# The two output tiles of a weight chunk: tile by tile, or in turn at every matmul

## The reference

```
proj = xn @ w_in                                  # 2048 x 4096, and w_o 2048 x 2048
h = gelu(conv(xn @ w_g)) * (xn @ w_u)             # 2048 x 6144 each, in both layers
f = h @ w_d                                       # 6144 x 2048, in both layers
```

## Time and profile before

| what | value |
|---|---|
| three runs | 2781.56, 2787.35, 2787.73 us (median 2787.35) |
| the profiled execution, first to last instruction | 2787.2 us |
| PE busy | 2630.7 us, 94%, 20425 matmuls |
| PEld busy | 2488.0 us, 89%, 20425 loads |
| DVE busy | 1648.2 us, 59% |
| ACT busy | 1121.7 us, 40% |
| chain that ended last | PE 85%, of it L1513, L1514 and L1515 24% each |

### The profile page before, as it was taken

How to read it: one execution, slowest core, us unless ns; L and a number is a source line. 1 busy time by engine, 2 the same in 40 slices (tenths; PEclk the granted TensorE clock), 3 DMA queues, 4 the chain that set the end, 5 groups by cost and what they waited for, 6 DMA issues and landing times.

```text
span 2787.2 us, 54670 instructions
## 1 busy us (share of the span) xinstructions
PE 2630.7 (94%) x20425; PEld 2488.0 (89%) x20425; DVE 1648.2 (59%) x2583; ACT 1121.7 (40%) x1531; POOL 252.7 (9%) x337
## 2 busy tenths in 40 slices
PE   5988979999999999997889999996999999999998
PEld 5988979999999999997886556896999999999997
DVE  5889567654666466648642214448665566556655
ACT  4366344443443344435423222334443344334433
POOL 1043130000000000022300000022000000000012
PEclk9999989999999999998989999998999999999999
DMA  6534535555555555553413330152555555555552
GB/s 202 182 126 147 187 121 159 181 183 180 180 180 182 180 177 180 181 168 108 120 55 110 94 106 17 64 179 96 185 180 180 179 179 180 183 176 179 180 185 75
DMA packets 435802, 425.46 MB, mean 153 GB/s; under 512 B 37308, under 2 KB 424468, under 8 KB 435432
## 3 DMA queue, kind: packets, MB, share of 16 engines
q1 hardware_dynamic: 432088, 415.63, 47.8%
q0 software_dynamic: 3200, 6.06, 0.7%
q10 hardware_dynamic: 432, 2.66, 0.3%
HBM read 420.86 MB, written 3.95 MB: 152 GB/s over the span
## 4 chain that ended last, share of the span: by engine, by line
PE 85%; DVE 8%; issue 3%; POOL 2%; ACT 1%; SPq 0%; DMA 0%; DVEq 0%; POOLq 0%; ACTq 0%
PE acc L1513 24%; PE acc L1514 24%; PE acc L1515 24%; PE mis L1750 2%; PE mis L1772 2%; DVE lo L1002 2%; DVE f L1224 2%; DVE ssum L1014 1%; PE acc L1740 1%; PE mis L1751 1%; ACT hi L693 1%; PE mis L1821 1%; DVE xnl L1031 1%; PE mis L1820 1%; POOL aa L614 0%
## 5 line engine op out<-in xcount | busy, mean ns | idle before, releaser
L1002 DVE TENSOR_TENSOR lo<-raw,hi 128x1024 fp32r<-128x1024 f32 x752 | 908.4, 1224 | 830.0 <-ACT hi L693 829.1
L693 ACT ACTIVATE hi<-raw 128x1024 fp32r<-128x1024 f32 x752 | 786.2, 1055 | 930.8 <-PE acc L1515 928.7
L1513 PE MATMUL acc<-xnh,hi 128*128 128x264 f32 x3664 | 1057.3, 289 | 65.7 <-issue 29.8
L1515 PE MATMUL acc<-xnh,lo 128*128 128x264 f32 x3664 | 1053.3, 287 | 0.0
L1514 PE MATMUL acc<-xnl,hi 128*128 128x264 f32 x3664 | 1051.7, 287 | 0.0
L1513 PEld LDWEIGHTS acc<-xnh,hi 128*128 128x128 f32 x3664 | 703.9, 192 | 71.6 <-issue 47.0
L1514 PEld LDWEIGHTS acc<-xnl,hi 128*128 128x128 f32 x3664 | 703.8, 192 | 0.4
L1515 PEld LDWEIGHTS acc<-xnh,lo 128*128 128x128 f32 x3664 | 699.3, 191 | 0.0
L1513 PE MATMUL acc<-hh,hi 128*128 128x264 f32 x2112 | 602.3, 285 | 0.0
L1515 PE MATMUL acc<-hh,lo 128*128 128x264 f32 x2112 | 602.2, 285 | 0.0
L1514 PE MATMUL acc<-hl,hi 128*128 128x264 f32 x2112 | 601.1, 285 | 0.0
(11 more groups left out here) (292 smaller groups left out, 2242.6 us busy)
## 6 DMA issues: line engine op xcount, KB each, us to landing
raw<-in_w_ffn_g SPq DMA_DIRECT2D x192, 512.0 KB, 4.5
raw<-in_w_ffn_u SPq DMA_DIRECT2D x192, 512.0 KB, 4.3
raw<-in_w_ffn_d SPq DMA_DIRECT2D x192, 512.0 KB, 3.7
raw<-in_w_rg_in SPq DMA_DIRECT2D x64, 512.0 KB, 5.1
raw<-in_w_rg_o SPq DMA_DIRECT2D x32, 512.0 KB, 4.6
cpage<-in_cache_kv_latent SPq DMA_DIRECT2D x64, 256.0 KB, 2.5
raw<-in_w_mla_o SPq DMA_DIRECT2D x32, 512.0 KB, 3.4
raw<-in_w_dkv SPq DMA_DIRECT2D x8, 512.0 KB, 4.6
```

Of the source, the lines that this page charges most:

```text
L693: act.activation(hi[:, c % SPLIT, :, 0:n], raw[:, c % RAW, :, 0:n], ACT.Copy).then_inc(s.hi_ready, 1)
L1002: dve.tensor_tensor(lo[:, c % SPLIT, :, 0:n], raw[:, c % RAW, :, 0:n], hi[:, c % SPLIT, :, 0:n].bitcast(F32), ALU.subtract).then_inc(s.lo_ ...
L1513: pe.matmul(out, wh, xh, start=start, stop=False)
L1515: return pe.matmul(out, wl, xh, start=False, stop=stop)
```

## The change

The three passes are written out in `group`, and the loop over the two output tiles becomes the innermost. The same 24 matmuls are issued for a chunk, with the same weights, activations and banks, and for each bank in the same order; only how the two tiles' matmuls are interleaved differs. The calls of `mm3` outside `group` stay as they are.

```
-                    for m in range(tiles):
-                        for k in range(4):
-                            kk = 4 * q + k
-                            w = (slice(None), slot, k, slice(m * P, m * P + P))
-                            last = mm3(acc[2 * (g % 2) + m][:, 0:T], hi[w], lo[w], xh[:, kk, :], xl[:, kk, :],
-                                       start=kk == 0, stop=kk == 4 * n - 1)
+                    for k in range(4):
+                        kk = 4 * q + k
+                        for n_pass, (half, moving) in enumerate(((hi, xh), (hi, xl), (lo, xh))):
+                            for m in range(tiles):
+                                w = (slice(None), slot, k, slice(m * P, m * P + P))
+                                last = pe.matmul(acc[2 * (g % 2) + m][:, 0:T], half[w], moving[:, kk, :],
+                                                 start=kk == 0 and n_pass == 0,
+                                                 stop=kk == 4 * n - 1 and n_pass == 2)
                     last.then_inc(s.chunk_used, 1)
```

## The result

| | median us | lowest to highest | runs |
|---|---|---|---|
| before | 2787.35 | 2781.56 to 2787.73 | 3 |
| changed | 2801.33 | 2799.72 to 2801.99 | 3 |

The changed kernel is slower by about 0.5%: ratio 1.0054, 95% interval 1.004 to 1.0068. That is 14.0 us more. I had forecast no change (2787 us) with 0.62, and slower with 0.17; the time lies inside the range that I gave (2770 to 2808).

The account below looks back on a forecast made before the run. TensorE's own matmul rate, 121.6 ns each, was taken to bound the kernel; 2787.2 us span + 0 + 0 + 0 gave 2787 us. Likeliest case 2779 to 2796, 8 in 10 range 2770 to 2808.

Parts of the forecast that it names:

- no change: Whole kernel: a time within 0.3% (8.4 us) of before, predicted as 2787 us; chance 0.62.
- slower: Whole kernel: more than 0.3% slower, by a worse pairing (0.15) or a falling clock (0.02); chance together 0.17.
- What bounds the kernel: Feed-forward stretches: only TensorE's rate counts, 121.6 ns per matmul, without gaps or waits, at clock 1.00.
- Instructions and waits at 0: Chunks in `group`: 17,568 matmuls and as many weight loads stay, no wait moves; cost 0.
- Bank switches at 0: Within chunks: 16,104 further bank switches cost 0, with -18 and +3 us kept as bounds.
- The three places: Bank evidence: a chunk's two existing switches, the float32 gate matmuls, and `value_pair`, which never switches; none showed a bank effect.
- Repeated weights at 0: L1513 to L1514: loading the same weights again saves nothing, so losing the repetition costs 0; at most 4 us gain.
- Which load lies beside which stream, at 0: Within chunks: new pairing of weight loads with streams taken as 0, bounded by -13 to +21 us.
- the two alternating patterns: Distances between matmul starts repeat every second chunk; both patterns sum to 2916 or 2917 ns, read as a stable mean.
- The worse pairing: Tile 1's weight load beside tile 0's stream makes each matmul 122.7 ns: +21 us, 2808 us; chance 0.15.
- The sum: Whole kernel: span 2787.2 us plus three zeros gives 2787 us, the span being 0.15 us from the median.
- The read ports: TensorE: by the skill's two independent read ports, loading weights takes no read bandwidth, so pairing would do nothing; 0.

Follow-up runs that it names:

- e1_bank: Kernel before, its order of weights and activations kept, but the bank alternates at each matmul; 2788.19 us, ratio 1.0003.
- e2_order: Changed kernel's order of weights and activations, but a chunk's first twelve matmuls write bank 0 and the last twelve bank 1; 2800.28 us, ratio 1.0051.
- e5_weights_new: Kernel before with weights loaded in the changed kernel's order, activations and banks as before; 2786.86 us, ratio 1.0002.
- e14_mpk96: Kernel before with loops reordered to tile, pass, k innermost, and all activation buffers 96 bytes further; 2763.79 us, ratio 0.9917.
- e10_mpk: Kernel before with loops reordered to tile, pass, k innermost, so the stream's address changes at every matmul; 2784.72 us, ratio 1.0001.
- e4_old64: Kernel before with all activation buffers 64 bytes further, weight buffers unmoved; 2778.38 us, ratio 0.9968.
- e8_all64: Kernel before with every buffer, weights and activations alike, 64 bytes further; 2786.37 us, ratio 1.0.
- e9_fixed: Kernel before, but all 24 streams of a chunk read the same activation tile; 2797.16 us, ratio 1.0043.
- e3_new128: Changed kernel with all activation buffers 128 bytes further, weight buffers unmoved; 2797.79 us, ratio 1.004.

## Why the prediction was wrong

*What bounds the kernel.* Right for the steady stretches: TensorE's rate is all there is, no wait moved, and the clock stayed at 1.00. A change of 1 ns per matmul shows there in full. Outside them I expected no change, but the attention stretch, whose code is untouched, came out 3.9 us shorter.

*Instructions and waits at 0.* Right: same counts, same waits.

*Bank switches at 0.* Right, and now shown by e1_bank and e2_order. The three places that I read before the run all pointed there. At the second I misread the clock. I set its 222 ns against 264 columns "at 1.2 GHz", but the clock was at its upper level in that stretch; at the lower level the same gate matmuls lie 440 ns apart. These are the stretch of the earlier trace rows and one at the lower level:

```profile
173.70:177.30 3.60, 3.60 (x18) 1.00 0.89 284
150.50:154.00 3.50, 3.46 (x8) 0.50 0.45 150
```

So a plain float32 matmul of 264 columns takes 222 ns at the full clock, about twice the 110.0 ns that I counted for 264 columns. That the seven switches there cost nothing stands.

*Repeated weights at 0.* Right: e5_weights_new takes the repetition away and costs nothing.

*Which load lies beside which stream, at 0.* This is the step that failed. The term measured +23.3 ns per chunk, some 17.0 us, where I had put 0; and what moved it was the sequence of the activations' start addresses, not the pair of load and stream. My bounds of -13 to +21 us held for this change (e14_mpk96, at 120.3 ns per matmul, lies outside them), but I took 0 from the middle. The reason that I gave was that the mean is "stable" because the two alternating patterns come to the same sum. Nothing makes them do so: under the same order 64 bytes further they are 2890.9 and 2922.5 ns. Two equal sums of one layout were one observation, not two. The earlier trace rows was the better witness: two short chunks at 122.7 and 120.7 ns that have the same order and read the same activation tiles. Its spread, up to 1% either way, should have been read as the likely size of the effect, and not as an edge, and the chance of no change should have been well under 0.62.

The same chunks also show what the address sequence leaves unexplained. Query chunks 4 and 8 read the same activation tiles, and their weights lie in the same slot; they begin behind different other work of TensorE. Their second and last matmuls:

```profile
1361.57 0.29 PE L1514 MATMUL acc<-cql,hi 128*128 128x264 f32 x1
1364.27 0.28 PE L1515 MATMUL acc<-cqh,lo 128*128 128x264 f32 x1
1377.67 0.28 PE L1514 MATMUL acc<-cql,hi 128*128 128x264 f32 x1
1380.35 0.28 PE L1515 MATMUL acc<-cqh,lo 128*128 128x264 f32 x1
```

From the unrounded starts that is 122.7 and 121.8 ns per matmul. So in a short chunk the addresses alone don't fix the distances; perhaps it is the state in which a chunk begins, which no run tests.

*The worse pairing, as a rival.* Its sign was right and its size near (slower, 2808 us, measured 2801.33), but that was luck. Its mechanism, tile 1's weights 512 bytes away beside tile 0's stream, was wrong: the order of the weights doesn't matter (e5_weights_new); all weight tiles begin at the same address modulo 256. What mattered is the sequence in which the streams' start addresses come, here six in a row at one address instead of three. The length of the stay isn't the cost by itself: with one in a row (e10_mpk) the time is that of before.

*The sum.* I took the span for the time. A run's time is 1.7 us more than its span (2801.99 against 2800.3 us), so the execution that was profiled before took some 2788.9 us, above the median. That is too little to matter here.

*The read ports.* The Trainium skill ("TensorE: Matmul & The Clock Gate", section "Step-by-step: what each phase is for") says that loading the next weights takes nothing from the running matmul's reads. If a load left the running matmul alone altogether, e4_old64 and e8_all64 could not differ in the way they do: moving the activations against the weights made the kernel 0.32% faster, moving both changed nothing. So for these fp32r operands at the full clock the measurement decides against the 0 that I read from it. Whether it is the bandwidth of the reads that a load takes, or something else, no run shows.

## What to carry to other kernels

If TensorE alone bounds a kernel and the starts of its matmuls lie unevenly in a repeating pattern, the order of the loops and the byte offset of the streamed buffer are a knob that was worth up to 1% here, and I found no way but a run to tell which way it turns: a reordering that touches neither waits nor counts isn't free. Measure order and offset together, since what one is worth depends on the other. And alternate accumulation banks for other reasons than speed; at 264 columns of these operands it did nothing.

## What the runs showed that I had not expected

- The distance between matmul starts depends on where the streamed fp32r activations begin relative to the weight buffers: from 120.0 ns to 126.7 ns at a fixed address (e9_fixed), 120.3 ns (e14_mpk96) to 122.5 ns (changed) on average over whole patterns.
- It has a memory: a run at one address needs about seven matmuls to settle, and on the way can be slower than at either end (131.8 ns at an address that settles at 120.0, in e9_fixed).
- 128 bytes exchange the two kinds of chunk exactly (e3_new128), and two chunks, 8448 bytes or 33 x 256, bring the pattern back.
- At the lower clock none of it shows: 0.22 us flat in the earlier trace rows.
- What in the chip links load and stream stays open. No run tells it, nor why 11.5 ns above the 110.0 ns of the columns are the usual value and 10.3 ns the best of these layouts.
